# The trunk as one stage, without barriers between its parts: three input tiles inside the end of attention, decay products ahead of the value products

## The reference, cut to what matters

```python
z = split_columns((rmsnorm(x, pre_g) * (1 + scale) + shift) @ w_in)      # 'zc' alike, of the context
y_mla = attention(...) * silu(z['mla_gate'])
# pool branch
mixed = einsum('blgi,gio->blgo', multiscale_pool(z['pool_x']), pool_w)   # windows of 2, 4, 8, 16 tokens
y_pool = mixed * pool_scale * silu(z['pool_gate'])
# linear attention (gla)
log_a_f = log_sigmoid(z['gla_af'] @ af_w2 + af_b) / 16                   # 'log_a_b' alike
o = chunked scan over q = z['gla_q'], k = z['gla_k'], v = z['gla_v'] with the running sums of log_a
y_gla = rmsnorm(o, g) * silu(z['gla_gate'])
# merge
gates = sigmoid(z['merge'])                                              # three gates of 1024
merged = g_mla * (y_mla @ w_bm) + g_pool * (y_pool @ w_bp) + g_gla * (y_gla @ w_bg)
x = x + gate * rmsnorm(merged @ w_out, post_g)
```

## Time and profile before

| | us |
|---|---|
| three runs | 1570.69, 1573.66, 1574.66 (median 1573.66) |
| the profiled execution | 1576.58, its span 1574.8 |
| TensorE busy | 1392.7 (88% of the span) |
| VectorE busy | 860.0 (55%) |
| GpSimd busy | 730.3 (46%) |
| ScalarE busy | 637.9 (41%) |

### The profile page before, as it was taken

One profiled execution on the slowest core, in us unless ns is written; L12 is line 12 of the kernel. 1 busy time (PEld: TensorE's weight loads), 2 busy tenths in 40 slices (PEclk: granted clock), 3 DMA queues, 4 the chain that ended last, 5 costly groups with the idle time before them and its releaser, 6 DMA issues.

```text
span 1574.8 us, 24551 instructions
## 1 busy us (share of the span) xinstructions
PE 1392.7 (88%) x10288; PEld 1164.0 (74%) x10288; DVE 860.0 (55%) x1213; ACT 637.9 (41%) x1002; POOL 730.3 (46%) x512
## 2 busy tenths in 40 slices
PE   5898899999999999688889699979799888799996
PEld 1654588677777787373777689968688777799996
DVE  1566605351333340756687565659889635488811
ACT  2445332342322323446424464556422123565542
POOL 0520044323213554050494866747745204499983
PEclk8899999999999999899999899989899999999998
DMA  8320033244335432130333333525222123355552
GB/s 342 109 67 14 28 94 100 66 148 170 106 114 207 142 100 80 32 115 14 109 118 104 112 107 122 167 85 179 94 82 82 55 83 114 96 179 186 185 177 80
DMA packets 48830, 179.73 MB, mean 114 GB/s; under 512 B 5457, under 2 KB 6481, under 8 KB 48337
## 3 DMA queue, kind: packets, MB, share of 16 engines
q1 hardware_dynamic: 48576, 176.08, 34.3%
q10 hardware_dynamic: 144, 2.10, 0.3%
HBM read 177.11 MB, written 1.05 MB: 113 GB/s over the span
## 4 chain that ended last, share of the span: by engine, by line
PE 62%; DVE 22%; ACT 7%; DMA 3%; POOL 3%; issue 3%; ACTq 0%; DVEq 0%; SPq 0%
PE ps L367 16%; PE ps L371 15%; PE ps L368 15%; PE ps L369 15%; DMA panels<-weights 3%; DVE work L1776 2%; POOL panels_r L411 1%; POOL panels_r L412 1%; ACT panels_hi L401 1%; PE ps L879 1%; DVE work L1220 1%; DVE small L926 1%; DMA const_sb<-constants 1%; DVE work L1174 1%; DVE work L988 1%
## 5 line engine op out<-in xcount | busy, mean ns | idle before, releaser
L411 POOL TENSOR_TENSOR panels_r<-panels,panels_hi 128x512 fp32r<-128x512 f32 x254 | 368.5, 1451 | 823.5 <-ACT panels_hi L401 822.1
L368 PE MATMUL ps<-h_sb_r,panels_hi 128*128 128x256 f32 (+1 forms) x1408 | 455.3, 323 | 0.0
L401 ACT ACTIVATE panels_hi<-panels 128x1024 fp32r<-128x1024 f32 x254 | 267.2, 1056 | 420.6 <-PE ps L369 251.2
L412 POOL TENSOR_TENSOR panels_r<-panels,panels_hi 128x512 fp32r<-128x512 f32 x254 | 375.0, 1476 | 0.0
L367 PE MATMUL ps<-hi_sb_r,panels_hi 128*128 128x512 f32 (+1 forms) x784 | 280.3, 358 | 32.9 <-DVE h_sb_r L613 14.0
L368 PEld LDWEIGHTS ps<-h_sb_r,panels_hi 128*128 128x128 f32 x1408 | 278.4, 198 | 18.4 <-issue 1.2
L369 PE MATMUL ps<-hi_sb_r,panels_r 128*128 128x512 f32 (+1 forms) x784 | 274.6, 350 | 0.0
L367 PEld LDWEIGHTS ps<-hi_sb_r,panels_hi 128*128 128x128 f32 x784 | 154.8, 197 | 58.6 <-DVE h_sb_r L613 15.3
L367 PE MATMUL ps<-h_sb_r,panels_hi 128*128 128x256 f32 x624 | 184.6, 296 | 12.3 <-DVE h_sb_r L594 7.6
L367 PE MATMUL ps<-work_r,panels_hi 128*128 128x256 f32 (+1 forms) x560 | 183.1, 327 | 11.5 <-POOL panels_r L412 7.4
L369 PE MATMUL ps<-h_sb_r,panels_r 128*128 128x256 f32 x624 | 180.4, 289 | 0.0
(11 more groups left out here) (321 smaller groups left out, 1825.1 us busy)
## 6 DMA issues: line engine op xcount, KB each, us to landing
panels<-weights SPq DMA_DIRECT2D x326, 512.0 KB, 3.5
x_sb<-x_in SPq DMA_DIRECT2D x1, 2048.0 KB, 8.3
x_sb<-x_in ACTq DMA_DIRECT2D x1, 2048.0 KB, 8.7
const_sb<-constants SPq DMA_DIRECT2D x1, 1216.0 KB, 10.8
out<-x_sb SPq DMA_DIRECT2D x2, 512.0 KB, 2.9
vec_sb<-vectors SPq DMA_DIRECT2D x1, 725.0 KB, 12.1
small<-c_in SPq DMA_DIRECT2D x1, 8.0 KB, 1.6
```

What stands on the lines that cost most here:

```text
L368: pe.matmul(o, lhsT.hi, rhs.lo, start=False, stop=False)
L401: act.activation(panels_hi[:, m:m + PANEL * P], panels[:, n:n + PANEL * P], ACT.Copy).then_inc(panel_rounded, 1)
L411: pool.tensor_tensor(panels_r[:, at:at + half], panels[:, at:at + half], panels_hi[:, m:m + half], ALU.subtract)
L412: pool.tensor_tensor(panels_r[:, at + half:at + 2 * half], panels[:, at + half:at + 2 * half], panels_hi[:, m + half:m + 2 * half], ALU.su ...
```

## The change

All parts of both layers and what follows become one stage behind the start, so that eight of the nine barriers go; waits on semaphores (`lat_scaled`, `front_taken`, and the counts of those that take the tiles) stand in their place. `projection` hands its functions back instead of adding a stage, and `trunk` places them:

- Input tiles 0, 1 and 2 run on TensorE in the last three iterations of attention, each ahead of that iteration's transposes; the rest stand behind attention. VectorE's side of all tiles stays behind its last product of attention.
- The decay products stand ahead of the value products, in banks 4 to 7, without the wait for a minimum. The weights for them move to a panel of their own. ScalarE takes the sizes before it copies its values and computes Exp and Ln behind them; VectorE takes the minima (into `la_first`) before turn 6, `split_y` and its value copies.
- Values use banks 1, 2, 3, 0, pool products banks 2, 0, 1, 3, and wait for the copies of the values instead of for the gates.
- Mix 0 (layer 0), mixes 0 and 1 (layer 1) stand between the scans, one behind the first and one behind the second.
- The turns: 0 to 2 behind tile 3, 3 behind tile 9, 4 behind tile 10, 5 behind tile 11, 6 behind the minima.
- `attn` is cleared (L1471, now L1519) ahead of VectorE's input tiles.

```diff
@@ stream_plan
+        add(f"gla_w{l}", [[part("gla_af_w2", l, 0, 16, m * P, P)] for m in range(2)]
+            + [[part("gla_ab_w2", l, 0, 16, m * P, P, 16)] for m in range(2)])
         add(f"gla_v{l}", [[part("w_in", l, k * P, P, IN_AT["gla_v"] + n * P, P)] for k in range(KD) for n in range(4)],
             split=True)
         add(f"pool_w{l}", [[Piece("pool_w", (l, g), False, 0, 0)] for g in range(len(WINDOWS))])
-        add(f"gla_w{l}", [[part("gla_af_w2", l, 0, 16, m * P, P)] for m in range(2)]
-            + [[part("gla_ab_w2", l, 0, 16, m * P, P, 16)] for m in range(2)])
...
@@ attn_tensor
+                blocks.mark("attention", l)
+                pe.wait_ge(*up_by_act)
+                pe.wait_ge(*up_by_dve)
                 for i in range(n_items + 3):
+                    if i >= n_items:
+                        pe.wait_ge(expd, i0 + min(i - 1, n_items))
+                        head_products(pe, i - n_items, i - n_items + 1)
...
@@ trunk
-                                               ("vector", 1): s5_factors, ("vector", 3): s5_turns(0, 2), ("vector", 9): s5_turns(2, 3),
-                                               ("vector", 10): s5_turns(3, 4), ("vector", 11): s5_turns(4, 5)} if last else {})
-            inputs = stages.pop()
+                                               ("vector", 1): s5_factors, ("vector", 3): s5_turns(0, 3), ("vector", 9): s5_turns(3, 4),
+                                               ("vector", 10): s5_turns(4, 5), ("vector", 11): s5_turns(5, 6)} if last else {})
+
+            def head_tensor(pe):
+                pe.wait_ge(expd, i0 + n_items)
+                head_products(pe, 3, 6)
+                pe.wait_ge(gated, p0 + n_items // 2)
+                head_products(pe, 6, 17)
...
+            return joined(front, up, attention, linear, out_part, next_part), next_ready
...
@@ gla_and_merge
                     if i >= 2:
                         pe.wait_ge(mixed, m0 + i - 1)
+                    else:
+                        pe.wait_ge(w_min, wm0 + 2 * i + 2)
...
             def decay_products(pe):
+                inputs.decay_banks_free(pe)
                 for i in range(4):
-                    if i == 3:
-                        pe.wait_ge(w_min, wm0 + 1)
-                    blocks.product(pe, ps[:, i % 3, 0:TOK], blocks.lhs(pe, plan[f"gla_w{l}"] + i), ga, True, True, w_filled)
...
+                    blocks.product(pe, ps[:, 4 + i, 0:TOK], blocks.lhs(pe, plan[f"gla_w{l}"] + i), ga, True, True, w_filled)
...
                 for i in range(4):
                     step(dve.tensor_tensor_scan(su[:, i, :], const("carry"), la[:, row_of[i], :], 0.0, ALU.mult, ALU.add))
+                    if i < 3:
+                        mixes(dve, i, min(i + 1, MIXES[l][0]))
...
             def tensor(pe):
+                inputs.head.tensor(pe)
                 decay_products(pe)
+                inputs.value_products(pe)
+                inputs.pool_products(pe)
                 items(pe, 0, cut[0])
...
             def scalar(act):
+                inputs.head.scalar(act)
                 round_y(act, 0)
-                decay_scalar(act)
+                decay_sizes(act)
+                inputs.values_scalar(act)
+                decay_logs(act)
...
             def vector(dve):
                 steps["dve"](dve.memset(attn, 0.0))
+                inputs.head.vector(dve)
+                decay_minima(dve)
+                if inputs.turns is not None:
+                    inputs.turns(6, 7)(dve)
                 split_y(dve, 0)
+                inputs.values_vector(dve)
+                inputs.pools_vector(dve)
                 decay_vector(dve)
-                mixes(dve, 0, MIXES[l][0])
+                mixes(dve, 3, MIXES[l][0])
```

105 lines of the change are left out of this document (62 added, 43 removed).

## The result

| | before | after |
|---|---|---|
| median of five runs, us | 1571.92 (1567.99 to 1574.66) | 1561.32 (1556.96 to 1564.30) |
| profiled execution, us | 1576.58 | 1564.30 |
| its span, us | 1574.8 | 1562.5 |

The ratio is 0.9914, with a 95% interval of 0.9892 to 0.9936. So the change is faster, by 10.6 us between these medians and 13 to 18 us by the ratios, where 7.0 were forecast. The time lies in the stated range, but the gain is one and a half to two and a half times the forecast one. A difference of a few us between two single traces can therefore be chance.

What follows compares the result with a forecast made beforehand. TensorE, busy 88% of the span, was taken as the bound, through idle time and lower clock. Terms -0.2 - 2.8 - 4.7 + 0.7 = -7.0 took 1576.58 to 1569.6, less 2.9 for the median: 1566.7 us, range 1560 to 1572.5.

Steps and rivals of the forecast that it cites:

- Barriers alone: All seams between stages: semaphores still hold most of the work, so removing barriers gives -0.2 us, between 0 and -0.8.
- Layer 0, tiles in the tail: End of attention in layer 0: three pool tiles fill TensorE's waits of 1.70, 0.56 and 0.56 us, -2.8 us.
- Layer 0, decays: Layer 0: decay products on four free banks ahead of the values, without the minimum's wait, -4.7 us, between -3.5 and -5.5.
- Layer 1, input stage: Layer 1 up to the values' end: tail waits filled, but stalls at tiles 4 and 10 make the values 13.2 us later.
- Layer 1, behind the values: Layer 1, from values to item 4: 25.5 us instead of 38.0, so -12.5; item 2 at 12.7 instead of 27.9.
- (c): Layer 1, end of values: VectorE is late, its windows taking 5 us more, so copies and scans too: 1571.7 us; chance 0.15.
- (d): Layer 1: turns 4 and 5 starve GpSimd as 2 and 3 do, kernel becomes slower, 1576.9 us; chance 0.07.
- (e): Layer 1, tile 4: no stall, because ScalarE is done earlier; 8 to 10 us less, 1558 us; chance 0.05.
- (f): Layer 0: filling the tail only moves the wait to a panel, leaving only -4.7 there, 1569.5 us; chance 0.05.

## Why the prediction was right and where it was wrong

**The step that failed: layer 0, in two terms.** The sum has -7.7 up to the end of layer 0 (-0.2, -2.8, -4.7), and the traces show -12.6. The term for the barriers was -0.2 and measured -1.7 at the first scores already. For what runs behind the decay products the sum had nothing, and there it is -3.8. The two terms in between are nearly right, as shown below.

**Barriers alone: -0.2.** I counted only the gap between the last engine's end and TensorE's start, 0.1 us at a seam. I had looked for what ends TensorE's idle time at the seam and not two rows further, where the wait of 2.69 us ended by ScalarE had a table load of 1.28 us in it. Of the 1.7 us 1.4 are this wait. In layer 1 the load gave nothing in this pair of traces. In the medians the load alone is worth 3.9 us (1.1 to 6.8) in the kernel before, and all barriers 7.4, uncertain by about 5; in the traces of that pair it is 5.1 us by the end of layer 1. Beside the load, what is placed are 0.57 us at each end of attention; the rest stays open.

**The clock: a term that the sum lacked for layer 0.** I gave half-clock stretches to layer 1's long waits (+2.2 each) and none to the waits that go in layer 0. Behind the decays the two traces before have two stretches of half clock (3.4 us each, at 310 and 368), and the changed kernel has none between 161 and 406 us. That the first of them belongs to the decay waits is shown (three traces with, 13 without); for the second it is open. For the whole kernel the lists of the core give for before 1574.8 us at a mean of 0.946 and 1575.7 at 0.944, for after 1562.5 at 0.950 and 1559.1 at 0.952. Time lost against full clock, (1 - clock) x span, is then 85.0 and 88.2 before, 78.1 and 74.8 after: 10 of the 14.5 us between the mean spans. It is an upper bound, since a low clock under an idle TensorE costs nothing, and part of it can be chance: the same sum differs by 10 us between the fastest and the slowest of the 23 executions of the kernel before (75 and 85).

**Layer 0, tiles in the tail: -2.8.** From -1.7 to -4.5, so -2.8; right to the tenth, which is partly luck: the kernel without the tiles loses 0.9 us by the first merge mix and 3.8 by the last.

**Layer 0, decays: -4.7.** From -4.5 to -8.8, so -4.2, within the bounds. The size was right and half the reason wrong: not the place ahead of the values but the fourth bank and the missing barrier did it. The 72 matmuls behind them then gained 1.1 us more (18.0 to 16.8) from the clock, and on the way to -12.6 come some 2.7 more: waits for panels of 0.73 and 1.54 us became 0.72 and 0.46, and the second half-clock stretch is gone.

**Layer 1, input stage.** Tile 3 ended 6.0 us earlier against the start of the tail (5.5 forecast), the wait at tile 4 was 8.59 (8.4), tile 4 and tile 9 started 2.3 us later (2.5 and 2.3), tile 10 7.8 later (8.0), the values ended 11.9 later (13.2). These are shifts against -12.4, where layer 1's tail began; by the span's clock the values ended 0.6 us earlier than before, where the forecast had them some 5.5 later, and 4.7 of that miss is the better layer 0. The chain through angles, polar step, rounding and split, and the alternation of GpSimd and VectorE, were read rightly from the rows before. The halves of 5.4 us, 1.3 alone, again agree with the exclusive lock of the Trainium skill, "SBUF — State Buffer", section "SBUF: two separate sides".

**Layer 1, behind the values.** Item 2 came 12.9 us behind them (12.7), but ended by GpSimd, not by the mix; item 4 27.2 behind them (25.5), since two of the small operations of the exponents took 1.2 us each beside GpSimd (0.17 before, when GpSimd stood still), and panel waits of 1.91 and 1.12 us came in between. So -10.8 for -12.5. At item 4, where the forecast's account ends, layer 1 stands at +1.1; by its last mix it is +0.6 against the last mix of layer 0. That this comes so near +0.7 is partly luck: 1.3 us too much in the input stage and 1.7 too much behind the values cancel.

**Rivals.** (c) did not come: VectorE waited 5.0 us for the values, its windows took 19.8 us instead of 26.9. (d), (e), (f) did not come either. That layer 0 might give more than its idle time was in none of them, and it should have been the first.

## What to carry to other kernels

Read a barrier's price from the first wait behind it as well as from the one at it: a table load ahead of an instruction with two waits runs behind one of them. When stages are joined, look for what the end of a stage did on the side (here the rounding of two panels, worth 7 us by the middle). Price an idle stretch of TensorE at its length and again at the clock behind it, for those that go as for those that come: in the changed kernel the first tile behind the wait of 8.59 us took 5.2 us and the next 2.9. And hold a shift between two traces against the spread of one kernel's own executions, here 14 us between the ends of 23, before giving it a cause.

## What the runs showed of the hardware

- A wait that is long fulfilled can cost: with a second one ahead of an exponential, the wait for the first maximum became an instruction of its own ahead of the table load of 1.28 us, the load ran behind it, and TensorE's wait went from 1.29 to 2.62 us.
- GpSimd and VectorE alternated on long operations: four halves of a panel, alone 1.3 us each, took 5.48, 3.32, 5.44 and 5.44 us beside four turns, each ending about 1.1 us behind the end of a turn.
- Idle time and clock go together: all three traces with the wait of 2.46 us between decay products have a stretch of half clock within 0.7 us behind it, and none of the 13 traces without it has one there. With the waits taken away the stretch of some 40 us behind them ran at a clock of 1.00 instead of 0.96.
